# Moving part of an adaLN weight matrix from the mixer to a feed-forward stage, with its sums on the vector engine

## The reference

```
def ada_params(cvec, w, b):
    m = jax.nn.silu(cvec) @ w + b
    return m.reshape(cvec.shape[0], N_ADA, 1, D_MODEL)

def half_ffn(h, shift, scale, gate, g_pre, g_post, w13, w2):
    u = modulate_2(rmsnorm_2(h, g_pre), shift, scale)
    return h + 0.5 * gate * rmsnorm_2(swiglu(u, w13, w2), g_post)

h_lat = half_ffn(h_lat, ml[:, 0], ml[:, 1], ml[:, 2], g[0], g[1], w13_a[l], w2_a[l])
h_lat, h_ctx_new = token_mixing(h_lat, h_ctx, (ml[:, 3], ml[:, 4], ml[:, 5]), (mc[:, 3], mc[:, 4], mc[:, 5]), ...)
h_lat = half_ffn(h_lat, ml[:, 6], ml[:, 7], ml[:, 8], g[4], g[5], w13_b[l], w2_b[l])
```

## Time and profile before

| | |
|---|---|
| runs (3) | median 2330.95 us, 2325.32 to 2333.26 |
| profiled execution, its span from first to last instruction | 2324.5 us |
| what lies around the span in that execution | not recorded |
| PE busy | 1985.3 us, 85% |
| DVE busy | 956.0 us, 41% |
| ACT busy | 733.2 us, 32% |
| read from memory | 669.12 MB |
| chain that ended last | PE 49%, DMA 35%, DVE 10%, ACT 3% |

### The profile page before, as it was taken

The page is one execution under the profiler, slowest core; times in us unless marked ns, Lnnn a source line. Parts: engine busy times, 40 slices in busy tenths (PEclk is TensorE's granted clock), DMA queues, the critical chain, the costliest instruction groups (busy, mean ns, idle before and its releaser), DMA issues.

```text
span 2324.5 us, 29725 instructions
## 1 busy us (share of the span) xinstructions
PE 1985.3 (85%) x12534; PEld 1352.5 (58%) x12534; DVE 956.0 (41%) x1625; ACT 733.2 (32%) x1196; POOL 42.6 (2%) x47
## 2 busy tenths in 40 slices
PE   6999767777887887877788799989999899999997
PEld 3646313432332433442345299868999899785786
DVE  3544222221221221122533354567664645653486
ACT  4323211110110111112111144455654554543365
POOL 0000000000000000000000000000000000000010
PEclk9999898999989999898899999999999999999999
DMA  9977999999999999999999955535345455250430
GB/s 389 416 305 266 408 407 410 417 413 413 413 414 414 416 414 411 415 413 408 410 411 410 404 191 182 168 102 179 103 150 171 161 181 182 88 209 18 145 118 19
DMA packets 210436, 672.10 MB, mean 289 GB/s; under 512 B 11504, under 2 KB 134512, under 8 KB 152192
## 3 DMA queue, kind: packets, MB, share of 16 engines
q1 hardware_dynamic: 210304, 670.21, 75.0%
HBM read 669.12 MB, written 1.05 MB: 288 GB/s over the span
## 4 chain that ended last, share of the span: by engine, by line
PE 49%; DMA 35%; DVE 10%; ACT 3%; issue 1%; SPq 0%; POOL 0%; DVEq 0%; ACTq 0%
DMA ring<-in_w 25%; PE pb L231 11%; PE pb L232 11%; PE pb L233 11%; DMA ring<-in_w_a 6%; DVE WB L329 3%; DMA ring<-in_w_in 3%; PE pb L1840 3%; PE pb L770 2%; PE pb L1865 2%; ACT WB L323 1%; DMA ring<-in_w_mod 1%; PE pb L3146 1%; PE pb L1039 1%; DVE big L3522 1%
## 5 line engine op out<-in xcount | busy, mean ns | idle before, releaser
L329 DVE TENSOR_TENSOR WB<-ring,WB 128x1024 fp32r<-128x1024 f32 (+3 forms) x370 | 426.4, 1194 | 514.2 <-ACT WB L323 513.8
L323 ACT ACTIVATE WB<-ring 128x1024 fp32r<-128x1024 f32 (+3 forms) x370 | 361.7, 1027 | 809.2 <-DMA ring<-in_w_a 457.6
L231 PE MATMUL pb<-HH,WB 128*128 128x256 f32 (+1 forms) x1680 | 497.3, 296 | 14.8 <-DVE WB L329 4.3
L232 PE MATMUL pb<-HL,WB 128*128 128x256 f32 (+1 forms) x1680 | 486.8, 290 | 0.0
L233 PE MATMUL pb<-HH,WB 128*128 128x256 f32 (+1 forms) x1680 | 486.4, 290 | 0.0
L1840 PE MATMUL pb<-ring,big 128*32 128x512 f32 x2048 | 297.7, 672 | 149.5 <-DMA ring<-in_w 134.2
L231 PEld LDWEIGHTS pb<-HH,WB 128*128 128x128 f32 x1680 | 333.7, 199 | 41.4 <-issue 22.9
L232 PEld LDWEIGHTS pb<-HL,WB 128*128 128x128 f32 x1680 | 333.5, 198 | 2.2 <-issue 2.1
L233 PEld LDWEIGHTS pb<-HH,WB 128*128 128x128 f32 x1680 | 333.0, 198 | 0.0
L1840 PEld LDWEIGHTS pb<-ring,big 128*32 128x32 f32 x2048 | 46.6, 114 | 364.2 <-DMA ring<-in_w 281.4
L1865 PE MATMUL pb<-ring,big 128*32 128x512 f32 x1024 | 160.7, 646 | 44.9 <-DMA ring<-in_w 36.3
(11 more groups left out here) (461 smaller groups left out, 1939.8 us busy)
## 6 DMA issues: line engine op xcount, KB each, us to landing
ring<-in_w SPq DMA_DIRECT2D x384, 1024.0 KB, 16.5
ring<-in_w_a SPq DMA_DIRECT2D x66, 1024.0 KB, 13.3
ring<-in_w_in SPq DMA_DIRECT2D x38, 1024.0 KB, 10.1
ring<-in_w_ada SPq DMA_DIRECT2D x36, 1024.0 KB, 9.9
ring<-in_w_b SPq DMA_DIRECT2D x33, 1024.0 KB, 5.0
ring<-in_w_mod SPq DMA_DIRECT2D x24, 1024.0 KB, 11.4
ring<-in_w_out SPq DMA_DIRECT2D x8, 1024.0 KB, 6.0
ring<-in_b_w_in SPq DMA_DIRECT2D x8, 1024.0 KB, 6.8
```

What stands on the lines that cost most here:

```text
L231: pe.matmul(o, l[0], r[0], start=start, stop=False)
L232: pe.matmul(o, l[0], r[1], start=False, stop=False)
L323: act.activation(WB[:, c % 2, 0, x:y], flat[:, x:y], ACT.Copy).then_inc(*A(("high", c, z)))
L329: dve.tensor_tensor(WB[:, c % 2, 1, x:y], flat[:, x:y], WB[:, c % 2, 0, x:y].bitcast(F32), ALU.subtract).then_inc(*V(("low", c, z), *([("f ...
```

## The change

w_ada's columns 0 to 5119 (vectors 0 to 4) stay ahead of the experts: panels ("ada", 0), ("ada", 1) and TWO, 20 units in place of 36. The steps are cut by the table FILL and to 1 in `values`. The columns of vectors 5 and 8 (b = 0) and of 6 and 7 (b = 1) are loaded in fa, 8 late units each, one after 2 of 3 chunks from chunk 1 to 23 (LATE_AT). The first late unit of each b is held, and DVE adds the others onto it in place: each late unit is two halves of 128 x 1024, multiplied by the latent condition's column (`dve_late`), one half after each chunk of the pair stage and a second one after odd pairs, and five more in the row stage. PE then sums the slot over its partitions with a block of ones (`pe_late_sum`), ACT copies (`act_late`), PE picks (`pe_late_pick`) and DVE adds bias and norms (`dve_late_out`): for b = 0 in pairs 7 to 10, for b = 1 in the row stage. PE waits for ACT's copy in the second bank of pair 8, and for DVE's result in that of pair 10.

The diff, cut to its core:

```diff
-    ADA = [("ada", nb) for nb in range(5)]
-    TWO = ("ada", 4)
+    ADA = [("ada", nb) for nb in range(3)]
+    TWO = ("ada", 2)
+
+    FILL = (1, 1, 2, 2, 2, 2, 2)
...
-                    load(sp, (v, u), w[256 * u:256 * u + 256, 8192:9216].rearrange("(a p) n -> p a n", p=128), 2048, "p (a n) -> p a n", a=2)
+                    load(sp, (v, u), w[256 * u:256 * u + 256, 4096:5120].rearrange("(a p) n -> p a n", p=128), 2048, "p (a n) -> p a n", a=2)
...
+    def late_half(i):
+        return i // 16, i // 2 % 8, i % 2
+
+    def late_columns(b, u):
+        w = I["w_ada_2"][0][128 * u:128 * u + 128, :]
+        return w[:, 6144:8192] if b else w[:, 5120:9216].rearrange("p (a n) -> p a n", n=1024)[:, 0:4:3, :]
+
+    def sp_late(sp, k):
+        b, u = divmod(k, 8)
+        if b:
+            load(sp, ("late", b, u), late_columns(b, u), 2048, hold=u == 0)
+        else:
+            load(sp, ("late", b, u), late_columns(b, u), 2048, "p (a n) -> p a n", hold=u == 0, a=2)
+
+    def dve_late(dve, n):
+        for i in range(n, min(n + 1, 32)):
+            b, u, z = late_half(i)
+            total, part = (slot(("late", b, x))[:, 1024 * z:1024 * z + 1024] for x in (0, u))
+            if z == 0:
+                dve.wait_ge(*landed(("late", b, u)))
+            if u == 0:
+                dve.tensor_scalar(total, total, cs[:, 1, 0, 0:1], None, ALU.mult).then_inc(*V(("late", b, u, z)))
+                continue
+            dve.wait_ge(*at("late", b, u - 1, z))
+            dve.scalar_tensor_tensor(total, part, cs[:, 1, u, 0:1], total, ALU.mult, ALU.add).then_inc(
+                *V(("late", b, u, z), *([("free", ("late", b, u))] if z else [])))
+
+    def late_bank(b):
+        return PB[4] if b else PB[3]
+
+    def pe_late_sum(pe, b):
+        pe.wait_ge(*at("late", b, 7, 1))
+        pe.wait_ge(*(at("silu", "fa", 9, 0) if b else at("glu", "fa", 6, 1)))
+        for j in range(4):
+            e = pe.matmul(late_bank(b)[32 * j:32 * j + 32, :], ones[:, 0:32], slot(("late", b, 0))[:, 512 * j:512 * j + 512],
+                          start=True, stop=True)
+        e.then_inc(*P(("late_sum", b), ("free", ("late", b, 0))))
+
+    def pe_late_pick(pe, b):
+        pe.wait_ge(*at("late_raw", b))
+        if b == 0:
+            pe.wait_ge(*at("glu", "fa", 8, 1))
+        for i in range(4):
+            e = pe.matmul(late_bank(b)[:, 8 * i:8 * i + 8].rearrange("p (j c) -> p j c", c=2), mraw[:, 128 * i:128 * i + 128],
+                          ident.rearrange("p (j c) -> p j c", j=4)[:, :, 0:2], start=True, stop=True)
+        e.then_inc(*P(("late_pick", b)))
+
+    def pe_late_last(pe):
+        for _ in range(4):
+            yield
+        pe_late_sum(pe, 1)
+        yield
+        yield
+        pe_late_pick(pe, 1)
+        yield
+
+    def act_late(act, b):
+        act.wait_ge(*at("late_sum", b))
+        if b:
+            act.wait_ge(*at("late_pick", 0))
+        act.activation(mraw[:, :], late_bank(b)[:, :], ACT.Copy).then_inc(*A(("late_raw", b)))
+
+    def dve_late_out(dve, b):
+        dve.wait_ge(*at("late_pick", b))
+        for c, j0, nj in ((48, 0, 4),) if b else ((40, 0, 2), (64, 2, 2)):
+            dve.tensor_tensor(mcol2[:, c:c + 4 * nj, :].rearrange("p (j i) c -> p i j c", i=4),
+                              late_bank(b)[:, 0:32].rearrange("p (i j c) -> p i j c", i=4, c=2)[:, :, j0:j0 + nj, :],
+                              col("b_ada_2", c, 4 * nj).rearrange("p (j i) -> p i j", i=4)[:, :, :, None].to_broadcast([128, 4, nj, 2]),
+                              ALU.add).then_inc(*V(*([("late_out", b)] if c != 40 else [])))
+        dve.wait_ge(*at("late_out", b))
+        if b:
+            dve.scalar_tensor_tensor(AB2[:, 32:40], mcol2[:, 56:64, 0], 1.0, ng(4), ALU.add, ALU.mult).then_inc(*V())
...
             load_chunk(sp, q + 1)
             if q:
-                steps(g2, 3)
+                steps(g2, FILL[q - 1])
...
-            steps(g2, 3)
+            steps(g2, FILL[3 + q])
...
         def values(t):
-            steps(g2, 2)
+            steps(g2, 1)
...
+    LATE_AT = {1 + 3 * k // 2: k for k in range(16)}
+
     def sp_half(sp, F):
         R.place("gr_" + F.name, True, 0)
         for c in range(F.s0 + 1, F.s0 + 34):
             load_chunk(sp, c)
+            if F is fa and c - F.s0 in LATE_AT:
+                sp_late(sp, LATE_AT[c - F.s0])
+            if F is fa and c - F.s0 in (18, 28):
+                R.let_go(("late", (c - F.s0) // 28, 0))
...
+                    if F is fa and (q, f) == (1, 1) and p in (8, 10):
+                        pe.wait_ge(*at("late_raw" if p == 8 else "late_out", 0))
...
+            if F is fa and p == 7:
+                pe_late_sum(pe, 0)
+            elif F is fa and p == 9:
+                pe_late_pick(pe, 0)
...
+                between=(lambda g=pe_late_last(pe): steps(g, 1)) if F is fa else None)
...
+            elif F is fa and p == 8:
+                act_late(act, 0)
...
+            if F is fa and n == 13:
+                act_late(act, 1)
...
+                if F is fa and (p, q) == (10, 0):
+                    dve_late_out(dve, 0)
+                if F is fa:
+                    dve_late(dve, late_n)
+                    late_n += 1
+                    if q and p % 2:
+                        dve_late(dve, late_n)
+                        late_n += 1
...
+            if F is fa and n % 2 == 0 and late_n < 32:
+                dve_late(dve, late_n)
+                late_n += 1
+            if F is fa and n == 19:
+                dve_late_out(dve, 1)
```

More of the change, by code:

```diff
@@ new lines, in pe_late_last @@
+    def pe_late_last(pe):
[21 more added lines that the diff above has]
+            dve.scalar_tensor_tensor(AB2[:, 32:40], mcol2[:, 56:64, 0], 1.0, ng(4), ALU.add, ALU.mult).then_inc(*V())
+        else:
+            dve.tensor_tensor(AB2[:, 56:64], mcol2[:, 40:48, 0], ng(3), ALU.mult).then_inc(*V())
+            dve.scalar_tensor_tensor(AB2[:, 64:72], mcol2[:, 64:72, 0], 0.5, ng(5), ALU.mult, ALU.mult).then_inc(*V())
@@ L1943, in dve_ada_scales @@
         dve.wait_ge(*at("mcol", TWO))
-        for i, (g, ch, which) in enumerate(((0, 1, 0), (0, 1, 1), (2, 4, 0), (2, 4, 1), (4, 7, 0))):
+        for i, (g, ch, which) in enumerate(((0, 1, 0), (0, 1, 1), (2, 4, 0), (2, 4, 1))):
             dve.scalar_tensor_tensor(AB2[:, 8 * i:8 * i + 8], mcol2[:, 8 * ch:8 * ch + 8, which], 1.0, ng(g), ALU.add, ALU.mult).then_inc(*V())
@@ L1947, in dve_ada_scales @@
             dve.scalar_tensor_tensor(AB2[:, 40 + 8 * i:48 + 8 * i], mcol2[:, 8 * ch:8 * ch + 8, which], 0.5, ng(g), ALU.mult, ALU.mult).then_inc(*V())
-        dve.tensor_tensor(AB2[:, 56:64], mcol2[:, 40:48, 0], ng(3), ALU.mult).then_inc(*V())
-        dve.scalar_tensor_tensor(AB2[:, 64:72], mcol2[:, 64:72, 0], 0.5, ng(5), ALU.mult, ALU.mult).then_inc(*V(("ab_2",)))
     def dve_experts(dve, sp_, g2):
@@ L2206, in pe_half @@
         pe_rows(pe, name, F.nt, 22, F.s0 + 22, [2 * i for i in range(F.nt)], lambda n: rb(n, T_), lambda i: 128 * i,
-                lambda n: [("lowR", name, n)], waits=lambda i, j: [("glu" if i else "silu", name, 10, j)])
+                lambda n: [("lowR", name, n)], waits=lambda i, j: [("glu" if i else "silu", name, 10, j)],
+                between=(lambda g=pe_late_last(pe): steps(g, 1)) if F is fa else None)
     def act_half(act, F, sp_):
@@ L2254, in rows @@
                 yield from dve_row(dve, F.rows[z], F.gates[z], F.tmp[0], [("row", F.rows[z - 1], 1)] if z else [])
-        gen = rows()
+        gen, late_n = rows(), 0
         for p in range(11):
```

## The result

| | before | changed |
|---|---|---|
| median, 9 runs each | 2330.95 us (2325.32 to 2335.7) | 2346.07 us (2338.54 to 2356.01) |
| ratio | 1 | 1.0077, 95% interval 1.0063 to 1.009 |
| span of the profiled execution | 2324.5 us | 2344.6 us |

The account below looks back on a forecast made before the run. PE was taken to set the pace ahead of the experts and in fa, transfers in the experts. Gain 15.3, cost 3.8 + 12.3 + 1.7 (clock) = 17.8, net +2.5 us: 2333.5 us, 8-in-10 range 2321 to 2343.

Parts of the forecast that it names:

- (a) and (b): First and second projection: fewer units on a busy PE, 3.7 us and 2.3 us gained.
- (c): Eight value steps: cut to one unit each, 8.0 us gained.
- Part 1: Ahead of the experts: 52 units become 36, 15.3 us gained in sum.
- (d): Routing: six units become four, 1.3 us gained; the first expert load moves with PE.
- Part 2: Added work in fa: two sums and two picks on PE, 3.8 us; VectorE's halves 1.25 us each.
- Part 3: Slots of the load ring in fa, held by sums and late units: PE waits of 12.3 us in sum.
- A: fa, second bank of the ninth pair: PE waits 4.2 us for ScalarE's copy behind chunk 18's split.
- B: fa, chunk 21: it lands late behind a late unit's slot, PE waits 2.25 us.
- C: fa, chunk 23 around the start of the row stage: PE waits 1.4 us.
- D: fa, chunk 24 in the row stage: it waits for unit 13's slot, PE waits 4.2 us.
- the front keeps its time: Rival: VectorE and pick waits ahead of the experts leave a gain of 5, not 15.3; 2343.7 us, chance 0.09.
- In time: Rival: slots in fa come free earlier, the four waits vanish; net -10.5, 2320.5 us, chance 0.15.

Follow-up runs that it names:

- E1: Changed kernel with every late unit loaded one chunk later in SyncE's order; 2329.48 us, ratio 0.9997.
- E2: Changed kernel without the late loads, halves, sums, picks and scales in fa; 2323.74 us, ratio 0.9971.
- E8: Changed kernel with ScalarE's copy of the first late sum ahead of its split of chunk 18; 2340.91 us, ratio 1.0038.
- E7: Changed kernel with the unit of each of the eight value steps issued twice, 32 more matmuls; 2341.27 us, ratio 1.0051.
- E10: Changed kernel without the late part, with two units in value steps 1 and 5 and two fewer in the routing; 2314.95 us, ratio 0.994.
- E4: Changed kernel with the units of value steps 1 and 5 issued twice; 2339.79 us, ratio 1.0034.
- E3: Changed kernel with two units in value steps 1 and 5 and two fewer in the routing; 2339.83 us, ratio 1.004.
- E5: Changed kernel with late loads one chunk later, two units in value steps 1 and 5, two fewer in the routing; 2316.89 us, ratio 0.9943.
- E11: Second run of the program of E5, on another chip; 2317.89 us, ratio 0.9954.

## Why the prediction was wrong, step by step

**(a) and (b), the projections: right.** 3.7 + 2.3 = 6.0 us forecast, 6.3 measured at the first score.

**(c), the value steps: the step that failed.** The forecast was 8.0 us gained, by taking the removed units off at the price that they had. It measured 4.5 us lost between the first score and the end of the steps, and 1.3 to 2.9 us lost in E1, E2 and E8, which have the same work there. The error is in "step 1 saves one unit, which ran at half clock ... but leaves the half clock to what follows, 0.9": I saw in the earlier trace rows that two units at half clock stood where the clock came back, and still priced the half clock as a fixed toll of some 3 us. As an estimate, with half of the low time taken off, the stage is 49.7 us before (54.7 - 5.0, from 137.25 to 191.99) and 38.9 after (59.0 - 20.1, from 131.21 to 190.17). The work would thus have given 10.8 us; the clock took 15.1. E7 shows that this work was free, E2 against E10 (6.6 and 14.0 us) that a second unit at two places, taken from the routing, returns half of Part 1. What is shown is that the clock depends on this work; how much of it brings the clock back, and why the same program gets 8 or 28 us, is open.

**(d) and the experts.** The routing's gain was undersized (1.3 us; 2.6 between the value steps and the first expert matmul). That matmul came 4.4 us sooner, 15.3 forecast; the first expert load did leave 11.4 us sooner (218.61 against 230.02 of the earlier trace rows), but only seven loads found a free slot, and the eighth left only at 243.74, when the first expert matmuls (from 241.75, 1.94 us) had used their slot. In the view of 210 to 245 us, with the eighth:

```profile
218.61 25.46 SPq L224 DMA_DIRECT2D ring<-in_w  x8
```

The load did not move with TensorE as forecast, and its earlier start was of little use. Nor did the gain carry through the experts. From the first expert matmul to the first of fa it is 1094.9 us before, 1097.4 in the changed kernel, 1092.9 to 1095.8 in E1, E2, E4, E7 and E8, and 1098.1 to 1099.7 in the six kernels with fewer units in the routing. So these six lose 3 to 5 us of their gain there, for a cause that no run here isolates.

**Part 2, fa's work: right in kind.** A late half takes 1.28 us (1.25 taken), 28 of them; the other four of the 32 begin a sum and are plain multiplications:

```profile
L840 DVE SCALAR_TENSOR_TENSOR ring<-ring,cs x28: 1275/1278/1286, 1355.1 to 1514.4; 128x1024 f32<-128x1024 f32 x28
```

Sums and picks were 3.8 us by forecast; E1, which has only those, is 4.9 longer in fa than before.

**Part 3, the ring: right in sum, 12.44 us against 12.3, with parts shifted.** A: 4.2 forecast, 4.06 measured, ended by ScalarE's copy, and E8 takes it away. B: 2.25 forecast, 4.44 measured; chunk 21 left 1.76 us behind the end of chunk 19, as forecast (1.7), but took 6.9 us to land where 5.0 was taken:

```profile
L224 SPq DMA_DIRECT2D ring<-in_w_a x1: 368/368/368, 1466.1 to 1466.1; - x1
...
DMA to landing us min/median/max: 6.9/6.9/6.9
```

C was absorbed by that longer wait. D: 4.2 forecast, 3.94 measured, and chunk 24 landed in 5.0. Here the estimate from the figure of the Trainium skill, DMA: Bandwidth & Descriptors, section Bandwidth (6.15 us for 1 MB), was nearer for B and farther for D.

**The clock in fa: undersized.** 1.7 us forecast for A and D together; all three waits bring some 3.4 us at the lower level, 5.1 us lost, of which 1.7 comes back because fa starts at half clock before and at full clock now (0.53 and 1.00 over its first 5 us). The 1.7 is an estimate; E10, whose fa starts at full clock, is 1.8 us shorter there than E2, whose fa starts at half clock. The Trainium skill, TensorE: Matmul & The Clock Gate, section HAM oscillation, has that waits between bursts of matmuls bring the half rate each time; in fa the traces agree in 13 waits of 14. The changed kernel has three of three, E3, E4 and E7 nine of nine, E8 one of two: behind its wait of 3.81 us, ended at 1488.80, the clock was 1.00 in every stretch of 2 us up to 1496. So "each time" does not hold here, and in E3 each wait brought some 6.7 us at the lower level (0.79 over the 16 us around each), with a fa of 219.6 us. For the larger loss the same page, section What's actually happening, has that being busy releases the throttle; the value steps differ, TensorE was busy 55.13 of 59 us there at a clock of 0.66, and the measurement decides.

**The sum.** In fa 12.4 (waits) + 5.1 - 1.7 (clock) + 4.9 (as in E1) make 20.7, measured 20.6, in place of 17.8; front 1.9 in place of 15.3 at fa's first matmul, 1.4 us more behind fa: 17.6 us between the spans' +20.1 and the forecast +2.5. One trace is not the whole answer. The traces with the same front (changed, E1, E2, E8) have fa's first matmul 1.9, 6.8, 7.5 and 9.0 us sooner than before, so the changed kernel's is the worst of four, and the 1.4 us behind fa are within what that stretch varies by (786.7 to 790.9 us). By medians the front gave 6.6 us in place of 15.3 and the late part cost 22.3 in place of 17.8, which makes +15.7 where +15.1 was measured. The prediction's own sign of being wrong, the experts ending less than 10 us sooner, came in all four. Of the rivals, "the front keeps its time" (2343.7, chance 0.09) came nearest, by another mechanism than the one it named: VectorE and the picks did not eat the gain. "In time" (0.15) was right that 16 loads fit into fa; it needed the other order of E1. "Against: the waits come from who frees a slot" holds for both.

## What to carry to other kernels

A unit of work that is taken out of a stage of small, dependent matmuls is worth its duration only if the clock of that stage doesn't hang on it: where a trace shows the granted clock coming back during just that work, price the stage at half clock without it, and try it with the work issued twice. In a queue that issues in order through a ring, an extra load is better placed near its own use than ahead of a chunk that is needed first; one place in the order was worth 16.6 us of 2346 here. And a stage that looks busier after work was removed is to be read by its clock, not by its busy share.

## What the runs showed of the hardware

Three things that I had not expected. TensorE issued 32 more matmuls of 128x512 in the value steps of E7 and the stage did not get longer (57 us against 56 to 59 in four traces without them), the clock being 0.87 in place of 0.66 to 0.70. And one program, E5 and E11, showed 28 and 7.5 us of low clock in the same stage in two executions, with spans of 2322.7 and 2315.3 us, so that one trace can't settle a question of the clock; the runs' medians with their intervals did. And a wait of TensorE of 2.7 to 5.2 us in dense work was followed by the half clock in 13 cases of 14, not in all.
